# Score stage: up blocks multiplied in native fp32 from the raw weights

## The chip, the cores and the metric

The kernel runs on one NeuronCore of a Trainium2 chip. The metric is the time of one execution in microseconds (us) on the device. Five engines work side by side, each on its own instruction stream: TensorE (PE: matmuls, with the weight loads PEld listed apart), VectorE (DVE), ScalarE (ACT), GpSimd (POOL) and SyncE (SP, which here issues the large DMAs). They meet at semaphores.

## The reference, cut to what matters

The program is one layer of a diffusion backbone on 128 context and 256 latent tokens: a token mixer (projection, bidirectional scan, output projection), then a channel mixer called PEER. Only PEER matters here:

```
q  = (h @ w_query)  as 8 heads x 2 halves x 128
s1 = q[:, :, 0] . sub_keys[0]      s2 = q[:, :, 1] . sub_keys[1]     # 128 scores per half
top 16 of each half, 16x16 sums, top 16 of the sums -> idx, gates = softmax(top)
act = gelu(x . expert_u[idx])      out = sum_k act * gate * expert_v[idx]
```

There are 16,384 experts of width 2048. For the 128 context tokens the kernel gathers the rows of the chosen experts. For the 256 latent tokens it computes the products with all experts densely (128 "up" blocks of 128 experts: `gelu(expert_u @ h)`), and weighs them with a table of gates that is zero where an expert was not chosen.

## The kernel before

The part around the change begins at line 1565. Its weights come as blocks of 128 x 2048 fp32 (1 MB), numbered m in the order of use. Each block goes through two-slot rings, slot r = m % 2: `raw` (as loaded), `whi` (its high part in fp32r, a rounded form that TensorE multiplies in one go) and `wlo` (raw minus whi, also fp32r). The activations h are kept three times: `h2` in fp32, `hhi` and `hlo` as high and low part. One 128x128 piece of a block is multiplied as whi x hhi + whi x hlo + wlo x hhi, three matmuls; 16 pieces make a block, so 48 matmuls (`up_product`, L1553 to L1559, for the 256 latent tokens; `query`, L1804 to L1816, for all 384 tokens).

The score stage is blocks 0 to 35. For each of 8 heads there are four blocks (`PER_HEAD`): query, query, up, up; the parity of a head's blocks is 0, 1, 0, 1. After them come `UPRE` = 4 further up blocks (32 to 35, from `M_PRE` on). So 16 query blocks and 20 up blocks. The next stage (the scatter stage, blocks 36 to 67, from `M_SCAT` on) builds the gate table; then the remaining up blocks run in a loop (`rest`), and the down blocks after them.

What sets the order in the score stage:

- SP (L1571 to L1605) loads block m into `raw[m % 2]` once the semaphore `w_low` of that slot says that block m-2 is done with (L1574). It then spills the gelu output of block m-3 to DRAM, if that was an up block, and goes on to block m+1. It is in order.
- ACT (L1679 to L1702) copies, per head m = 4h: the query result of block m, then makes `whi` of block m+2 (`high_of`, L1547); the result of block m+1, then `whi` of m+3; then `gelu` of block m+2, `whi` of m+4, the two score copies (L1696), `gelu` of m+3, `whi` of m+5. `high_of` waits for the load of its block and for the product of block m-2. In head 0, four copies of the turned tokens (`htok`, L1688) stand ahead of the first gelu. After the last blocks, ACT takes the Exp of the gates (L1704).
- POOL (L1951) makes `wlo` of blocks 0 to 35 in turn (`low_of`, L1542); its increment of `w_low` is what PE waits for before the product, and what SP waits for before it overwrites `raw`. After block 35 it waits for the chosen indices and starts the gathers of expert rows.
- PE (L1831 to L1852) runs query, query, up, the six score matmuls (L1844), up; each product waits for `w_low` of its block. After the last up block, PE waits for the gates and transposes them (L1854 to L1860).
- DVE runs `choose(h)` for each head (L2019 to L2056, the top-k work), which begins when the two score copies of the head are there; after head 7 it writes `idx` (L2066), waits for the Exp and normalises the gates (L2070 to L2074). The dots with gathered rows (L2082) and everything in the scatter stage follow.

Of the kernel before, what the change touches and what calls it, by code (L numbers as in the profile page):

```python
# [29 lines left out]
KD = D // P  # L30
CTX, LAT = 128, 256
T = CTX + LAT
# [126 lines left out]
def build_program(nc, x_t, c_t, cols_in, tables_in, w_ada, w_in, w2a2, w_s, b_s, state_t, w_out, w_query,  # L159
# [9 lines left out]
    with ctx:  # L169
        ps = ctx.enter_context(nc.psum_tensor("ps", [P, 8, 512], F32))  # L170
# [141 lines left out]
        raw = sb(b_scope, "raw", [P, RING, KD, P])  # L312
# [1003 lines left out]
        raw = stack_right(w_scope, "raw2", [P, RING, KD, P])  # L1316
# [120 lines left out]
        PER_HEAD = 2 + UPH  # L1437
        M_PRE = PKH * PER_HEAD
        M_SCAT = M_PRE + UPRE
        M_REST = M_SCAT + USCAT  # L1440
        M_DOWN = NQ + NK
# [39 lines left out]
        h2 = carve(fa_, KD, T)  # L1481
# [36 lines left out]
        w_landed = [sem(f"w_landed{r}") for r in range(2)]  # L1518
        w_high = sem("w_high")
        w_low = [sem(f"w_low{r}") for r in range(2)]  # L1520
        prod = sem("prod")
        q_out, u_out = sem("q_out"), sem("u_out")
# [16 lines left out]
        evicted, turned_back, added_back = sem("evicted"), sem("turned_back"), sem("added_back")  # L1539
        stores_y = sem("stores_y")  # L1540

        def low_of(eng, ops, m):  # L1542
            r = m % 2
            eng.wait_ge(w_high.sem, m + 1)
            ops.tensor_tensor(wlo[:, r], raw[:, r], whi[:, r].bitcast(F32), ALU.subtract).then_inc(w_low[r].sem, 1)  # L1545

        def high_of(act, m):  # L1547
            r = m % 2
            act.wait_ge(w_landed[r].sem, 16 * (m // 2 + 1))
            act.wait_ge(prod.sem, m - 1)  # L1550
            nc.scalar.activation(whi[:, r], raw[:, r], ACT.Copy).then_inc(w_high.sem, 1)
# [13 lines left out]
        with nc.Block() as block:  # L1565
# [100 lines left out]
            def _(act):  # L1666
                def gelu(m, g):
                    act.wait_ge(prod.sem, m + 1)
                    if g >= 2:
                        act.wait_ge(spilled[g % 2].sem, 16 * (g // 2))  # L1670
                    nc.scalar.activation(act_f[:, g % 2], ps[:, 2 + g % 2, 0:LAT], ACT.Gelu_apprx_tanh).then_inc(u_out.sem, 1)
# [7 lines left out]
                for h in range(PKH):  # L1679
                    m = h * PER_HEAD  # L1680
# [44 lines left out]
                for i in range(SCAT):  # L1725
                    m, g, q = M_SCAT + 2 * i, U_SCAT + 2 * i, QUADS * i
# [58 lines left out]
                for tile in range(2):  # L1785
                    for c in range(4):
                        act.wait_ge(sums_ready.sem, 4 * tile + c + 1)
                        last = nc.scalar.activation(vg[1 + tile][:, c * 512:(c + 1) * 512], ps[:, 4 * tile + c, :], ACT.Square,
                                                    accum_out=tok_part[:, tile, c:c + 1])
# [11 lines left out]
            def _(pe):  # L1801
# [14 lines left out]
                    last.then_inc(prod.sem, 1)  # L1816

                def up(m, g):
                    pe.wait_ge(w_low[m % 2].sem, m // 2 + 1)
                    if g >= 2:  # L1820
                        pe.wait_ge(u_out.sem, g - 1)
                    up_product(pe, m % 2, ps[:, 2 + g % 2, 0:LAT])
# [8 lines left out]
                for h in range(PKH):  # L1831
                    m = h * PER_HEAD
# [46 lines left out]
                for i in range(SCAT):  # L1879
                    m, g, q = M_SCAT + 2 * i, U_SCAT + 2 * i, QUADS * i  # L1880
# [58 lines left out]
            @block.gpsimd  # L1939
            def _(pool):  # L1940
                def gather(rows, s, buf, landed):
                    nc.gpsimd.indirect_dma_start(out=buf, out_offset=None, in_=rows,  # L1942
                                                 in_offset=bass.IndirectOffsetOnAxis(ap=idx[:, s:s + 1], axis=0)
                                                 ).then_inc(landed.sem, 16)

                def gather_u(s):
                    if s >= 2:
                        pool.wait_ge(ug_used.sem, s - 1)
                    gather(u_rows, s, ug[s % 2], ug_landed[s % 2])

                for m in range(M_SCAT):  # L1951
                    low_of(pool, nc.gpsimd, m)
                pool.wait_ge(x_saved.sem, 16)
                pool.wait_ge(idx_ready.sem, 1)
                for s in range(FIRST_DOTS):
                    gather_u(s)
                low_of(pool, nc.gpsimd, M_SCAT)
                low_of(pool, nc.gpsimd, M_SCAT + 1)
                pool.wait_ge(slots_here.sem, 1)

                def gate_two(q):
                    pool.wait_ge(fa_mask.sem, q + 1)
                    a = (4 * q) % 8 + 2
                    f = fa[:, a:a + 2, :]
                    nc.gpsimd.tensor_tensor(
                        f, f, slot[:, 0, 4 * q + 2:4 * q + 4].rearrange("p (t o) -> p t o", o=1).to_broadcast([P, 2, NK]),
                        ALU.mult).then_inc(fa_pool.sem, 1)

                gate_two(0)
                gate_two(1)  # L1970
                s = FIRST_DOTS
                for i in range(SCAT):
                    q = QUADS * i
                    gate_two(q + 2)
                    gate_two(q + 3)
                    for _ in range(SCAT_DOTS):
                        gather_u(s)
                        s += 1
                    if i < SCAT - 1:
                        gate_two(q + 4)  # L1980
                        gate_two(q + 5)
                    low_of(pool, nc.gpsimd, M_SCAT + 2 * i + 3)
                while s < SLOTS:
                    gather_u(s)
                    s += 1
                pool.wait_ge(stage_out[0].sem, 16 * (SCAT // 8))
                pool.wait_ge(stage_out[1].sem, 16 * (SCAT // 8))
                for s in range(SLOTS):
                    if s >= 4:
                        pool.wait_ge(vg_used.sem, s - 3)  # L1990
                    gather(v_rows, s, vg[s % 4], vg_landed[s % 4])

            @block.vector
            def _(dve):
# [122 lines left out]
                def rest(it):  # L2117
                    for n in range(4):
                        r = n % 2
                        dve.wait_ge(w_high.sem, it * 4 + (M_REST + 2 + n + 1))  # L2120
                        nc.vector.tensor_tensor(wlo[:, r], raw[:, r], whi[:, r].bitcast(F32), ALU.subtract).then_inc(w_low[r].sem, 1)  # L2121
                        u = (SLOTS - REST + n) % 2
                        dve.wait_ge(ug_landed[u].sem, it * 32 + 16 * ((SLOTS - REST + n) // 2 + 1))
                        nc.vector.scalar_tensor_tensor(out=ug[u], in0=ug[u], scalar=1.0, in1=htok[:, :], op0=ALU.mult,  # L2124
                                                       op1=ALU.mult, accum_out=dots[:, bass.ds(it * 4 + (SLOTS - REST + n), 1)]
                                                       ).then_inc(ug_used.sem, 1)
# [30 lines left out]
                                                   op0=ALU.mult, op1=ALU.add).then_inc(vg_used.sem, 1)  # L2157

                def v_low(it, j, e):
                    dve.wait_ge(w_high.sem, it * 4 + (M_DOWN + 2 * j + 2 + e + 1))  # L2160
                    nc.vector.tensor_tensor(wlo[:, e], v_raw[(2 * j + 2 + e) % 4], whi[:, e].bitcast(F32), ALU.subtract).then_inc(w_low[e].sem, 1)  # L2161

                def period(it, j, first=False):
# [111 lines left out]
```

## Time and profile before

| | before |
|---|---|
| median of 3 runs | 3718.75 us (3710.18 to 3724.95) |
| the profiled execution's own time | 3716.84 us |
| its span | 3715.0 us |
| PE busy | 3205.8 us (86%), 19560 instructions |
| PEld busy | 2821.9 us (76%) |
| DVE busy | 2501.2 us (67%) |
| ACT busy | 1426.1 us (38%) |
| POOL busy | 820.6 us (22%) |
| mean granted TensorE clock | 0.93 of full speed |

The span is the profiler's window around the instructions of the one profiled execution; the execution's own time is 1.84 us longer. The score stage lies between about 1705 and 2007 us. A matmul's row shows the time until its end leaves the array, and matmuls are pipelined: what one costs is the distance between two starts, not its duration. A native fp32 matmul shows as two records of a MATMUL and two of a LDWEIGHTS under one line of the source, an fp32r matmul as one of each.

### The profile page before, as it was taken

What the parts mean: (1) busy time and instruction counts of PE and PEld (TensorE: products, weight loads), DVE (VectorE), ACT (ScalarE), POOL (GpSimd) and SP (SyncE); (2) the same over time, 40 slices, a digit from 0 to 9 for tenths busy, and PEclk for the clock granted to TensorE, in tenths of its full rate; (3) what the DMA queues carried; (4) which work ended last, traced back from release to release, by engine and by line L of the source; (5) the groups of instructions that cost most, each with busy time, mean ns of one, the idle gap of its engine ahead of it and who ended that gap; (6) DMA issues with size and microseconds to landing.
All of it is one profiled execution on the core that took longest, in us unless ns stands there. A gap on an engine that the chain in (4) does not pass through costs nothing.

```text
span 3715.0 us, 52988 instructions
## 1 busy us (share of the span) xinstructions
PE 3205.8 (86%) x19560; PEld 2821.9 (76%) x19560; DVE 2501.2 (67%) x3095; ACT 1426.1 (38%) x1763; POOL 820.6 (22%) x469
## 2 busy tenths in 40 slices
PE   7988998949999999596996666569999799999997
PEld 2337998938888889494996666569999788788776
DVE  6985553365554452635997766667777699999997
ACT  6874333333334331425333333223333333333333
POOL 0000000001000010202565443331111234434442
PEclk9999999969999995798998888789999899999998
DMA  9983333200000000223445567779999999999996
GB/s 379 420 355 111 124 125 112 91 4 4 3 3 3 6 1 2 79 102 115 151 152 180 208 230 247 236 260 386 377 359 361 371 415 417 417 417 417 417 417 255
DMA packets 207375, 810.66 MB, mean 218 GB/s; under 512 B 81472, under 2 KB 101056, under 8 KB 118336
## 3 DMA queue, kind: packets, MB, share of 16 engines
q1 hardware_dynamic: 170432, 541.14, 38.9%
q0 software_dynamic: 36864, 268.45, 18.3%
q8 instruction: 51, 0.84, 0.1%
q14 instruction: 28, 0.23, 0.0%
HBM read 769.16 MB, written 40.37 MB: 218 GB/s over the span
## 4 chain that ended last, share of the span: by engine, by line
DMA 20%; DVE 13%; PE 12%; issue 4%; ACT 3%; POOL 1%; SPq 0%; DVEq 0%; ACTq 0%
DMA work<-act_table 10%; DMA raw<-expert_u 5%; DMA x<-u_rows,idx 4%; DVE x L2093 4%; PE ps L1556 2%; DVE x L2082 2%; PE ps L1558 2%; PE ps L1557 2%; DVE work L2156 2%; DVE wlo L2121 2%; ACT whi L1751 1%; PE ps L1813 1%; PE ps L1814 1%; PE ps L1815 1%; DVE wlo L2161 1%
## 5 line engine op out<-in xcount | busy, mean ns | idle before, releaser
L1556 PE MATMUL ps<-hhi,whi 128*128 128x256 f32 x2048 | 595.9, 291 | 32.5 <-DVE wlo L2121 14.9
L1557 PE MATMUL ps<-hlo,whi 128*128 128x256 f32 x2048 | 586.2, 286 | 0.0
L1558 PE MATMUL ps<-hhi,wlo 128*128 128x256 f32 x2048 | 585.3, 286 | 0.0
L1909 PE MATMUL ps<-whi,hhi 128*128 128x512 f32 x1024 | 402.0, 393 | 40.4 <-DVE wlo L2161 20.8
L1556 PEld LDWEIGHTS ps<-hhi,whi 128*128 128x128 f32 x2048 | 401.3, 196 | 41.2 <-issue 29.0
L282 PE MATMUL ps<-hhi,whi 128*128 128x384 f32 x1056 | 357.6, 339 | 79.0 <-DVE hlo L1413 42.9
L1557 PEld LDWEIGHTS ps<-hlo,whi 128*128 128x128 f32 x2048 | 400.6, 196 | 0.0
L1558 PEld LDWEIGHTS ps<-hhi,wlo 128*128 128x128 f32 x2048 | 399.7, 195 | 0.0
L1910 PE MATMUL ps<-wlo,hhi 128*128 128x512 f32 x1024 | 399.7, 390 | 0.0
L1911 PE MATMUL ps<-whi,hlo 128*128 128x512 f32 x1024 | 399.4, 390 | 0.0
L1942 POOL DMA_INDIRECT work<-expert_v,idx x128 | 287.2, 2244 | 445.5 <-DVE work L2156 430.5
L284 PE MATMUL ps<-hhi,wlo 128*128 128x384 f32 x1056 | 355.8, 337 | 0.0
L283 PE MATMUL ps<-hlo,whi 128*128 128x384 f32 x1056 | 355.7, 337 | 0.0
L1545 POOL TENSOR_TENSOR wlo<-raw,whi 128x2048 fp32r<-128x2048 f32 x54 | 251.4, 4658 | 329.5 <-ACT whi L1675 189.4
L2156 DVE SCALAR_TENSOR_TENSOR work<-work,dots 128x2048 f32<-128x2048 f32 x127 | 297.6, 2344 | 0.1
L271 DVE TENSOR_TENSOR wlo<-raw,whi 128x2048 fp32r<-128x2048 f32 x90 | 206.9, 2305 | 121.2 <-ACT whi L265 121.2
L282 PEld LDWEIGHTS ps<-hhi,whi 128*128 128x128 f32 x1056 | 200.7, 190 | 82.8 <-issue 56.7
L1909 PEld LDWEIGHTS ps<-whi,hhi 128*128 128x128 f32 x1024 | 192.9, 188 | 88.9 <-DVE wlo L2161 29.5
L2121 DVE TENSOR_TENSOR wlo<-raw,whi 128x2048 fp32r<-128x2048 f32 x76 | 174.2, 2292 | 124.0 <-ACT whi L1751 124.0
L1942 POOL DMA_INDIRECT x<-u_rows,idx x128 | 124.7, 975 | 524.7 <-DVE x L2124 390.4
L1876 PE MATMUL ps<-x 128*128 128x128 f32 x512 | 97.1, 360 | 162.1 <-DVE x L2093 142.4
L2082 DVE SCALAR_TENSOR_TENSOR x<-x,htok 128x2048 f32<-128x2048 f32 x52 | 134.6, 2590 | 140.4 <-DMA x<-u_rows,idx 140.4
(299 smaller groups left out, 6693.6 us busy)
## 6 DMA issues: line engine op xcount, KB each, us to landing
raw<-expert_u SPq DMA_DIRECT2D x128, 1024.0 KB
z<-w_ada SPq DMA_DIRECT2D x72, 1024.0 KB, 15.4
raw<-expert_v SPq DMA_DIRECT2D x64, 1024.0 KB
work<-expert_v SPq DMA_DIRECT2D x64, 1024.0 KB
raw<-w_in SPq DMA_DIRECT2D x50, 1024.0 KB, 4.8
raw<-w_ada SPq DMA_DIRECT2D x24, 1024.0 KB, 14.5
raw<-w_out SPq DMA_DIRECT2D x16, 1024.0 KB, 4.7
raw<-w_query SPq DMA_DIRECT2D x16, 1024.0 KB
```

Of the source, the lines that this page charges most:

```text
L282: pe.matmul(bank, hi[:, k, :], hhi[:, k, :], start=(k == 0), stop=False)
L283: pe.matmul(bank, hi[:, k, :], hlo[:, k, :], start=False, stop=False)
L284: last = pe.matmul(bank, lo[:, k, :], hhi[:, k, :], start=False, stop=(k == KD - 1))
L1545: ops.tensor_tensor(wlo[:, r], raw[:, r], whi[:, r].bitcast(F32), ALU.subtract).then_inc(w_low[r].sem, 1)
L1556: pe.matmul(bank, whi[:, r, k, :], moving_hi, start=(k == 0), stop=False)
L1557: pe.matmul(bank, whi[:, r, k, :], moving_lo, start=False, stop=False)
L1558: last = pe.matmul(bank, wlo[:, r, k, :], moving_hi, start=False, stop=(k == KD - 1))
L1909: pe.matmul(bank, ah, vh[:, part], start=first, stop=False)
L1910: done = pe.matmul(bank, ah, vl[:, part], start=False, stop=False)
L1911: done = pe.matmul(bank, al, vh[:, part], start=False, stop=last)
L1942: nc.gpsimd.indirect_dma_start(out=buf, out_offset=None, in_=rows, in_offset=bass.IndirectOffsetOnAxis(ap=idx[:, s:s + 1], axis=0)).then_i ...
L2156: nc.vector.scalar_tensor_tensor(out=accs[:, :], in0=vg[n], scalar=dots[:, bass.ds(it * 4 + n, 1)], in1=accs[:, :], op0=ALU.mult, op1=ALU. ...
```

## The change

A block for which `whole(m)` holds (the up blocks among blocks 0 to 31, and blocks 32 to 35: 20 in all) is multiplied straight from `raw` and `h2`, both fp32, in 16 native fp32 matmuls. For these blocks ACT makes no high part and POOL no low part. PE waits for the load itself (`w_landed`), and `w_low`, by which SP learns that the slot of `raw` is free, is incremented by ACT at the head of the block's gelu, after the product. The counts of `w_high` that other waits use are lowered accordingly. Query blocks and all blocks from 36 on are as before.

```diff
--- before.py
+++ after.py
@@ -1539,13 +1539,23 @@
         evicted, turned_back, added_back = sem("evicted"), sem("turned_back"), sem("added_back")
         stores_y = sem("stores_y")
 
+        def whole(m):
+            return M_PRE <= m < M_SCAT or (m < M_PRE and m % PER_HEAD >= 2)
+
+        WHOLE = sum(whole(m) for m in range(M_DOWN))
+
+        def highs(m):
+            return sum(not whole(n) for n in range(m + 1))
+
         def low_of(eng, ops, m):
             r = m % 2
-            eng.wait_ge(w_high.sem, m + 1)
+            eng.wait_ge(w_high.sem, highs(m))
             ops.tensor_tensor(wlo[:, r], raw[:, r], whi[:, r].bitcast(F32), ALU.subtract).then_inc(w_low[r].sem, 1)
 
         def high_of(act, m):
             r = m % 2
+            if whole(m):
+                return
             act.wait_ge(w_landed[r].sem, 16 * (m // 2 + 1))
             act.wait_ge(prod.sem, m - 1)
             nc.scalar.activation(whi[:, r], raw[:, r], ACT.Copy).then_inc(w_high.sem, 1)
@@ -1666,6 +1676,8 @@
             def _(act):
                 def gelu(m, g):
                     act.wait_ge(prod.sem, m + 1)
+                    if whole(m):
+                        act.sem_inc(w_low[m % 2].sem, 1)
                     if g >= 2:
                         act.wait_ge(spilled[g % 2].sem, 16 * (g // 2))
                     nc.scalar.activation(act_f[:, g % 2], ps[:, 2 + g % 2, 0:LAT], ACT.Gelu_apprx_tanh).then_inc(u_out.sem, 1)
@@ -1816,6 +1828,15 @@
                     last.then_inc(prod.sem, 1)
 
                 def up(m, g):
+                    if whole(m):
+                        pe.wait_ge(w_landed[m % 2].sem, 16 * (m // 2 + 1))
+                        if g >= 2:
+                            pe.wait_ge(u_out.sem, g - 1)
+                        for k in range(KD):
+                            last = pe.matmul(ps[:, 2 + g % 2, 0:LAT], raw[:, m % 2, k, :], h2[:, k, CTX:T],
+                                             start=(k == 0), stop=(k == KD - 1))
+                        last.then_inc(prod.sem, 1)
+                        return
                     pe.wait_ge(w_low[m % 2].sem, m // 2 + 1)
                     if g >= 2:
                         pe.wait_ge(u_out.sem, g - 1)
@@ -1949,7 +1970,8 @@
                     gather(u_rows, s, ug[s % 2], ug_landed[s % 2])
 
                 for m in range(M_SCAT):
-                    low_of(pool, nc.gpsimd, m)
+                    if not whole(m):
+                        low_of(pool, nc.gpsimd, m)
                 pool.wait_ge(x_saved.sem, 16)
                 pool.wait_ge(idx_ready.sem, 1)
                 for s in range(FIRST_DOTS):
@@ -2117,7 +2139,7 @@
                 def rest(it):
                     for n in range(4):
                         r = n % 2
-                        dve.wait_ge(w_high.sem, it * 4 + (M_REST + 2 + n + 1))
+                        dve.wait_ge(w_high.sem, it * 4 + (M_REST + 2 + n + 1 - WHOLE))
                         nc.vector.tensor_tensor(wlo[:, r], raw[:, r], whi[:, r].bitcast(F32), ALU.subtract).then_inc(w_low[r].sem, 1)
                         u = (SLOTS - REST + n) % 2
                         dve.wait_ge(ug_landed[u].sem, it * 32 + 16 * ((SLOTS - REST + n) // 2 + 1))
@@ -2157,7 +2179,7 @@
                                                    op0=ALU.mult, op1=ALU.add).then_inc(vg_used.sem, 1)
 
                 def v_low(it, j, e):
-                    dve.wait_ge(w_high.sem, it * 4 + (M_DOWN + 2 * j + 2 + e + 1))
+                    dve.wait_ge(w_high.sem, it * 4 + (M_DOWN + 2 * j + 2 + e + 1 - WHOLE))
                     nc.vector.tensor_tensor(wlo[:, e], v_raw[(2 * j + 2 + e) % 4], whi[:, e].bitcast(F32), ALU.subtract).then_inc(w_low[e].sem, 1)
 
                 def period(it, j, first=False):
```

## Rows read from the trace of the kernel before

**Rows 1.** A stretch of the score stage: length; PE, PEld, DVE, ACT, POOL busy.

```profile
1800.00:1850.00 50.00, 50.00 (x344) 49.67 (x343) 47.18 (x131) 16.80 (x18) 30.18 (x8) 1.00 0.40 134
```

**Rows 2.** Timeline of ACT, one head: start, duration, line, work, idle before.

```profile
1847.51 0.38 ACT L1671 ACTIVATE act_f<-ps 128x256 f32<-128x256 f32 x1 [3.45 <-PE ps L1558]
1847.79 1.91 ACT L1551 ACTIVATE whi<-raw 128x2048 fp32r<-128x2048 f32 x1
1849.60 0.86 ACT L1696 ACTIVATE work<-ps 128x384 f32<-128x384 f32 x2
1854.85 0.38 ACT L1671 ACTIVATE act_f<-ps 128x256 f32<-128x256 f32 x1 [4.39 <-PE ps L1558]
...
1877.24 0.38 ACT L1671 ACTIVATE act_f<-ps 128x256 f32<-128x256 f32 x1 [3.45 <-PE ps L1558]
```

**Rows 3.** Timeline of PE: second matmul of an up block, then the scores.

```profile
1747.11 0.28 PE L1557 MATMUL ps<-hlo,whi 128*128 128x256 f32 x1
...
1752.74 1.50 PE L1844 MATMUL ps<-work 128*128 128x128 f32 x12
```

**Rows 4.** Timeline of PE in the scan: native fp32 matmuls, 256 columns.

```profile
837.34 0.59 PE L1127 MATMUL ps<-kr,z 128*128 128x256 f32 x2
...
838.21 0.38 PE L1127 MATMUL ps<-kr,z 128*128 128x256 f32 x1
```

**Rows 5.** Timeline of PE: native fp32 matmuls of 384 columns, back to back.

```profile
1698.64 2.23 PE L1297 MATMUL ps<-z,tab 128*128 128x384 f32 x6 [0.21 <-ACT z L1289]
```

**Rows 6.** Timeline of SP: one 1 MB load is issued.

```profile
1832.04 0.33 SPq L1569 DMA_DIRECT2D raw<-expert_u  x1
```

**Rows 7.** Stretches of 1 us after that issue; last column is GB/s.

```profile
1836.00:1837.00 1.00, 1.00 (x8) 1.00 (x7) 0.95 (x5) 0.00 (x0) 1.00 (x1) 1.00 0.24 98
1837.00:1838.00 1.00, 1.00 (x8) 1.00 (x7) 0.91 (x3) 0.00 (x0) 1.00 (x1) 1.00 0.00 0
```

**Rows 8.** Timeline of POOL: a low part, after its high part.

```profile
1849.78 4.63 POOL L1545 TENSOR_TENSOR wlo<-raw,whi 128x2048 fp32r<-128x2048 f32 x1 [1.04 <-ACT whi L1551]
```

**Rows 9.** Timeline of ACT in head 0.

```profile
1754.71 1.09 ACT L1688 ACTIVATE htok<-ps 128x512 f32<-128x512 f32 x2 [5.13 <-PE ps L1828]
```

**Rows 10.** Timeline of PE: starts after an idle time.

```profile
1763.98 0.69 PE L1813 MATMUL ps<-hhi,whi 128*128 128x384 f32 x1 [3.12 <-POOL wlo L1545]
...
1994.25 0.39 PE L1556 MATMUL ps<-hhi,whi 128*128 128x256 f32 x1 [1.78 <-POOL wlo L1545]
```

**Rows 11.** Stretches of PE after these starts; PEclk is the granted clock.

```profile
1764.00:1766.80 2.80, 2.80 (x9) 0.50 0.66 161
...
1995.60:1999.00 3.40, 3.40 (x18) 0.51 0.78 303
```

**Rows 12.** Timeline of DVE: choose(6) ends, choose(7) runs, gates follow.

```profile
1959.76 1.83 DVE L2040 TENSOR_TENSOR work<-work,tab 128x768 f32<-128x768 f32 x2
...
1970.39 1.26 DVE L2005 MAX8 work<-work 128x8 f32<-128x128 f32 x6 [0.29 <-DVE second L2054]
...
1988.81 6.20 DVE L2040 TENSOR_TENSOR work<-work,tab 128x768 f32<-128x768 f32 x2
...
1999.59 0.23 DVE L2066 CAST idx<-dots 128x128 uint32<-128x128 f32 x1
2005.83 0.55 DVE L2070 TENSOR_REDUCE rstd<-gates 128x24 f32<-128x384 f32 x1 [6.02 <-ACT gates L1704]
```

**Rows 13.** Timeline of ACT, from the first up block of head 7 on.

```profile
1966.42 0.38 ACT L1671 ACTIVATE act_f<-ps 128x256 f32<-128x256 f32 x1 [3.45 <-PE ps L1558]
...
2001.79 0.38 ACT L1671 ACTIVATE act_f<-ps 128x256 f32<-128x256 f32 x1 [6.86 <-PE ps L1558]
2002.07 1.90 ACT L1551 ACTIVATE whi<-raw 128x2048 fp32r<-128x2048 f32 x1
2003.98 1.28 ACT L1704 ACT_TABLE_LOAD   x1
2005.28 0.52 ACT L1704 ACTIVATE gates<-gates 128x384 f32<-128x384 f32 x1
```

## The prediction, made before the changed kernel was run

> **What bounds the kernel now.** I read the page's slices first (the score stage lies at 1705 to 2007 us), then the stretches of 50 us, then the timeline of each engine over one head. In a stretch inside the stage PE is busy 50.00 of 50 us at full clock, DVE 47.18, ACT 16.80 and POOL 30.18 [rows 1]; the two stretches after it look the same. So PE sets the pace and DVE is close behind. One head lasts from gelu to gelu 1877.24 - 1847.51 = 29.73 us, of which the stretch from the first up block's end to the second's is 1854.85 - 1847.51 = 7.34 [rows 2].
>
> What a block costs is read from distances of starts. From the second matmul of an up block to the score matmuls are 47 distances in 1752.74 - 1747.11 = 5.63 us [rows 3], so 0.1198 us each and 5.75 for 48. A query block is half of the rest of the head, (29.73 - 7.34 - 5.75) / 2 = 8.32. Of the 7.34, 5.75 is the second up block and 1.6 the score matmuls and their hand-over.
>
> **The change, part by part.** I call T the moment at which ACT sees the first up block of a head finished (1847.51 in rows 2).
>
> 1. The product. 48 fp32r matmuls become 16 native ones of 256 columns, 32 records. The scan has them in this width: two matmuls (four records, each with its own weights loaded beside the running product) take 838.21 - 837.34 = 0.87 us, so 0.2175 a record [rows 4]. Six records of 384 columns take (2.23 - 0.59) / 5 = 0.328 each [rows 5] (0.59 is the duration of one such record in the same stretch; five distances make the rest), and twelve of 128 columns 0.111 [rows 3]: 0.85 to 0.87 ns a column at three widths. A block is 32 x 0.2175 = 6.96 us, 1.21 more than 5.75. The ends: 32 x 0.2175 from the row of the same width is the low one; each of the four passes as dear as an fp32r matmul, 4 x 0.1198 x 16 = 7.67, the high one. I take 6.96, the row of the same shape.
>
> The Trainium skill ("FP8 and Floating Point Precision", TensorE Precision Notes) says that true fp32 takes 4 passes through the array. By that rule, with a pass priced as the fp32r matmul that the block uses today, the block is the 7.67 above, and it would be 1.92 dearer instead of 1.21. The trace agrees with four passes but prices them lower, at 0.435 us for a matmul [rows 4].
>
> 2. ACT's high part (1.91 us [rows 2]) and POOL's low part (4.63 [rows 8]) go, 20 times. Both lie beside PE's work, and for the query blocks they stay. Gain: nothing on the path. Of POOL's work beside choose(7) more below.
>
> 3. The release of `raw`. This is the term that counts. Today SP may reload a slot as soon as the low part is made, long before the product; now a whole block holds its slot until its product is over, and ACT frees it. Both up blocks of a head are followed in their slots by the next head's query blocks, which still need load, high part and low part. The load: issued at 1832.04 [rows 6], still 98 GB/s in the microsecond from 1836 and nothing from 1837 [rows 7], so landed after 4.2 to 4.3; with the two hand-overs 4.4. ACT starts the high part, POOL starts 1.99 later (1849.78 - 1847.79 [rows 2, 8]) and takes 4.63. The first query block of the next head is thus ready at T + 4.4 + 1.99 + 4.63 + 0.1 = T + 11.1. PE has the scores and the second up block in front of it, 1.6 + 6.96 = 8.56: it stands idle for some 2.5 us, in every head but the last. Behind the waiting product on PE stand only the rest of the next head's work, on ACT the score copies: these now wait for the load and the high part (T + 6.4 in place of T + 2.1), and choose(h) begins 4.3 later in its head. DVE has the room for that, since the head gets longer by more.
>
> The second query block: its slot is free at T + 8.56, so it is ready at T + 19.66; PE ends the first at 11.1 + 8.32 = T + 19.42. A tie, 0.24 of idle time. Then 8.32 + 6.96 and 0.25 of hand-over: the head lasts 35.2 us, 5.5 more than 29.73.
>
> 4. The clock. After an idle time of 3.12 us the first query block of head 1 ran at a granted clock of 0.50 for 2.80 us [rows 10, 11]; after one of 1.78 the granted clock fell to 0.51 for 3.40 us, a little later [rows 10, 11]. Idle times of 2.5 lie between these. 2.8 us at half clock lose 1.4 us. In a head that has it, the first query block ends at T + 20.8, the tie of part 3 is gone, and the head lasts 20.8 + 8.32 + 6.96 + 0.25 = 36.35, 6.6 more. Ends for this part: 5.5 (no head loses) to 6.6 or, with two such stretches, 8.0. I take 6.6 in five heads and 5.5 in one.
>
> 5. Head 0. Here ACT frees the slot only after the last two `htok` copies, which end at 1754.71 + 1.09 = 1755.80 [rows 9], and these come 1.21 later for the dearer up block: 1757.0. The query block starts at 1757.0 + 11.1 = 1768.1, against 1763.98 [rows 10], and the clock is low after it in both. With 1.21 for the next up block, T of head 1 is 5.3 late.
>
> 6. The end of the stage. Seen from T of head 7 (1966.42), DVE begins to normalise the gates at 2005.83 [rows 12, 13], 39.4 later. There the chain is: last product, seen at 2001.79, a high part for block 37, the table load and the Exp [rows 13]. New: 1.6 + 5 x 6.96 = 36.4 for the product. The high part of block 37 stands ahead of the Exp on ACT, and its slot is free only now: 4.4 for the load, 1.95 for the high part, 1.28 + 0.55 for table and Exp: 44.6. That is 5.2 late. The whole blocks among these (32 to 35) need the load alone, which takes less than one product, so PE does not wait.
>
> choose(7) gets shorter: with POOL at work its two L2040 take 6.20 us, without 1.83 [rows 12]. It also begins sooner, so `idx` is there some 20 us before the gates. It buys little: the first dots stand behind the gates on DVE (2005.83 comes after `idx` at 1999.59 [rows 12]), and the gathers after the first two wait for the dots.
>
> Sum: 5.3 (head 0 and the up block after it) + 5 x 6.6 + 5.5 (heads 1 to 6) + 5.2 = 49.0 us. From the gates on, everything hangs on them or on `idx`; loads and gathers of the next stage stand to the gates as before, so I see nothing that takes the delay up. 3716.84 + 49.0 = 3765.8 for the profiled execution; the median of the runs stands 1.9 above that, so **3768 us**.
>
> **Rivals.**
>
> *Dearer passes or more half clock (slower still).* If a block is 7.67, 0.71 more, this adds 2 x 0.71 before head 1, 0.71 in each of six heads (the second up block lies under the reload) and 5 x 0.71 at the end: 9.2, so 3777. If each of seven stalls costs two half-clock stretches, 7 x 1.4 = 9.8: 3778. For it: a block reads h2 and raw in fp32, which no row shows in this stage, and rows 10 have a stretch of half clock after only 1.78 idle. Against it: three widths agree on the price. This is also the case of the skill's rule in part 1.
>
> *The reload is hidden.* If the slot came free early, or load and split took under 8.5 us together, only the arithmetic is left: 15 x 1.21 = 18.2 before T of head 7, and at the end 36.4 + 0.4 + 1.9 + 1.85 = 40.6 against 39.4: 1.2. Then 3718.75 + 19.4 = 3738. For it: PE has 8.56 us of work in front, and 2.5 is not much to be wrong by. Against it: load, high and low part are in series, each from a row.
>
> *DVE sets the pace (faster).* DVE is busy 47 of 50 us, and choose(7) begins 0.29 after choose(6), without a wait for the scores [rows 1, 12]. If the top-k chain is what holds each head, and PE's full rows only hide waiting, taking POOL's work from beside it gives back 6.20 - 1.83 = 4.4 a head, 8 x 4.4 = 35: 3684. It decides from the point where PE's head fits into DVE's, some 25 us. Against it: PE's head is 8.32 x 2 + 5.75 x 2 + 1.6 = 29.7 by its own starts, the whole period, and becomes 32.2 even without a stall. The Trainium skill ("SBUF — State Buffer", Who interferes with whom) calls the port pair that DVE and GpSimd share an exclusive lock, held for a whole instruction. The trace agrees, with 6.20 against 1.83, but on an engine that does not end last.
>
> **How the numbers follow.** Forecast 0.70; the slower-still case 0.17; hidden reload 0.08; DVE 0.03; something else 0.02, mostly slower. The forecast's own range is 3759 (no half clock at all, 43.5 less what the runs scatter) to 3775. To hold 8 in 10 it takes in the slower-still case and leaves the hidden reload out: 3746 to 3786. Half a per cent, 18.6 us, is about what a measurement here can tell from no change; the hidden reload lies just on that line and is shared out. Slower 0.92, same 0.05, faster 0.03.
>
> **What would show it.** Up products of 32 records at 0.2175 us, about 6.96 from start to start of their neighbours. PE idle about 2.5 us before the first query block of each head from 1 to 7 (5 us in head 1's case), ended by POOL's low part, whose high part was ended by a DMA on `raw`; SP's issues for those blocks right behind the gelu and not behind POOL. Heads of 35 to 36.5 us. A granted clock below 1.00 in the stage. DVE idle before each choose. ACT waiting for a load before the Exp. The stages after it as long as before. It is wrong if PE goes from the second up block straight into the next query block, if records of 256 columns stand far from 0.2175 apart, or if the scatter stage is shorter by what the score stage lost.

## The result and the profile after

The changed kernel takes 3770.09 us (median of 4 runs, 3753.49 to 3779.54) against 3714.47 for the kernel before on the same chips (4 runs, 3701.62 to 3724.95). The ratio is 1.0147, 95% interval 1.0097 to 1.0196, so slower by 36 to 73 us; 3768 had been forecast. That the two times lie 2 us apart is partly luck: the forecast added 49.0 us to a median of 3718.75, while the two medians here are 55.6 us apart and start from 3714.47. The profiled execution of the changed kernel is the slowest of its four (3779.54, span 3777.6). Its distance to the profile of before (62.6 us of span) is more than the distance of the medians, and the stages have to be read one by one.

L and a number is a line of the kernel that ran. In the changed kernel L1836 is the native product, L1825 the first matmul of a query piece, L1683 the gelu, L1561 and L1553 the high and the low part, L1579 the load, L1695 the copy of a query result.

The stretches of the score stage, in the order length; PE, PEld, DVE, ACT, POOL busy; granted clock, DMA share, GB/s (before: [rows 1]):

```profile
1800.00:1850.00 50.00, 43.50 (x218) 40.99 (x217) 36.06 (x139) 9.41 (x13) 18.14 (x4) 0.93 0.39 137
1850.00:1900.00 50.00, 46.41 (x251) 43.59 (x250) 37.34 (x131) 7.32 (x10) 9.19 (x3) 1.00 0.32 111
```

PE was busy all the time before; now it stands idle 3.6 to 6.5 us in 50, and DVE has room. ACT over one head (against [rows 2]):

```profile
1793.33 0.38 ACT L1683 ACTIVATE act_f<-ps 128x256 f32<-128x256 f32 x1 [6.50 <-PE ps L1836]
1798.12 1.91 ACT L1561 ACTIVATE whi<-raw 128x2048 fp32r<-128x2048 f32 x1 [4.41 <-DMA raw<-w_query]
1799.94 0.85 ACT L1708 ACTIVATE work<-ps 128x384 f32<-128x384 f32 x2
1801.58 0.38 ACT L1683 ACTIVATE act_f<-ps 128x256 f32<-128x256 f32 x1 [0.78 <-PE ps L1836]
1806.63 1.91 ACT L1561 ACTIVATE whi<-raw 128x2048 fp32r<-128x2048 f32 x1 [4.67 <-DMA raw<-w_query]
...
1830.17 0.38 ACT L1683 ACTIVATE act_f<-ps 128x256 f32<-128x256 f32 x1 [6.50 <-PE ps L1836]
```

The high part followed the gelu at once before (0.28 us from start to start [rows 2]). Now ACT waits 4.41 us for the load of the first query block, with the score copies behind it, and again 4.67 us for that of the second. The head lasts 1830.17 - 1793.33 = 36.84 us. The load on SP, then stretches of 1 us after it, then POOL and PE (against [rows 6, 7, 8, 10]):

```profile
1793.28 8.57 SPq L1579 DMA_DIRECT2D raw<-w_query  x2
```

```profile
1797.00:1798.00 1.00, 1.00 (x6) 0.90 (x5) 0.00 (x0) 0.00 (x0) 0.00 (x0) 1.00 0.32 131
1798.00:1799.00 1.00, 1.00 (x6) 0.87 (x6) 0.00 (x0) 0.88 (x1) 0.00 (x0) 1.00 0.00 0
```

```profile
1800.11 4.51 POOL L1553 TENSOR_TENSOR wlo<-raw,whi 128x2048 fp32r<-128x2048 f32 x1 [24.81 <-ACT whi L1561]
```

```profile
1804.68 0.44 PE L1825 MATMUL ps<-hhi,whi 128*128 128x384 f32 x1 [3.23 <-POOL wlo L1553]
...
1841.58 0.45 PE L1825 MATMUL ps<-hhi,whi 128*128 128x384 f32 x1 [3.28 <-POOL wlo L1553]
```

The chain is to be read as one line: ACT sees the first up block done at T = 1793.33, SP has issued the reload at 1793.28, ACT starts the high part at 1798.12 (4.8 later), POOL the low part 1.99 after that, and PE starts the query block at T + 11.35, after 3.23 us of idle time. The granted clock right behind it, on PE alone (length, PE busy, granted clock, DMA share, GB/s):

```profile
1804.70:1808.30 3.60, 3.60 (x12) 0.56 0.98 382
1808.60:1813.90 5.30, 5.30 (x32) 1.00 0.15 59
```

This half clock does not come in every head. Two heads later the start and the idle time are much the same, and the clock stays full (the row at 1914.31 is one head on, with half clock again):

```profile
1878.35 0.45 PE L1825 MATMUL ps<-hhi,whi 128*128 128x384 f32 x1 [3.11 <-POOL wlo L1553]
...
1914.31 0.69 PE L1825 MATMUL ps<-hhi,whi 128*128 128x384 f32 x1 [3.11 <-POOL wlo L1553]
```

```profile
1878.40:1882.00 3.60, 3.60 (x21) 1.00 1.01 394
```

Of the six heads, four ran the first query block at half clock at its start (at 1804.68, 1841.58, 1914.31 and 1951.06) and two did not (at 1878.35 and 1987.88). From its start to the copy of its result it took 10.2 us in the four and 8.6 in the two.

The end of the stage, on ACT (against [rows 13], where the last head's first gelu was at 1966.42 and the Exp at 2005.28). 2012.17 is the last head's first up block:

```profile
2012.17 0.38 ACT L1683 ACTIVATE act_f<-ps 128x256 f32<-128x256 f32 x1 [6.50 <-PE ps L1836]
...
2034.23 0.38 ACT L1683 ACTIVATE act_f<-ps 128x256 f32<-128x256 f32 x1 [6.53 <-PE ps L1836]
2041.14 0.38 ACT L1683 ACTIVATE act_f<-ps 128x256 f32<-128x256 f32 x1 [6.52 <-PE ps L1836]
2050.61 1.91 ACT L1561 ACTIVATE whi<-raw 128x2048 fp32r<-128x2048 f32 x1 [9.09 <-DMA raw<-expert_u]
2052.43 0.36 ACT L1683 ACTIVATE act_f<-ps 128x256 f32<-128x256 f32 x1
2055.78 1.91 ACT L1561 ACTIVATE whi<-raw 128x2048 fp32r<-128x2048 f32 x1 [2.99 <-DMA raw<-expert_u]
2057.71 1.28 ACT L1716 ACT_TABLE_LOAD   x1
2059.00 0.52 ACT L1716 ACTIVATE gates<-gates 128x384 f32<-128x384 f32 x1
```

Two loads now stand ahead of the Exp, 9.09 and 2.99 us of waiting. And POOL's first gather, which before followed `idx` at 1999.59 [rows 12], is issued while PE still has two blocks to go:

```profile
2038.05 1.15 POOL L1963 DMA_INDIRECT x<-u_rows,idx  x1 [41.55 <-DVE idx L2088]
2039.50 0.94 POOL L1963 DMA_INDIRECT x<-u_rows,idx  x1 [0.30 <-issue]
```

### The profile page after: what moved, and what is told of

The parts are those of the page before. It is cut to its first block, busy times and chain, and to the rows that moved or that the text cites. A ratio compares the mean times of both kernels' runs of the same rounds, so it can differ in the third digit from the quotient of the medians.

```text
span 3777.6 us, 52233 instructions
## 1 busy us (share of the span) xinstructions
PE 3237.1 (86%) x19240; PEld 2829.8 (75%) x19240; DVE 2469.4 (65%) x3095; ACT 1394.2 (37%) x1743; POOL 758.0 (20%) x449
## 4 chain that ended last, share of the span: by engine, by line
DMA 24%; DVE 12%; PE 9%; issue 4%; ACT 3%; POOL 2%; SPq 1%; DVEq 0%; ACTq 0%
DMA work<-act_table 10%; DMA raw<-expert_u 9%; DMA x<-u_rows,idx 4%; DVE x L2115 3%; PE ps L1836 3%; DVE wlo L2143 2%; DVE x L2104 2%; ACT whi L1763 2%; DVE work L2178 2%; DVE wlo L2183 1%; DMA raw<-w_query 1%; POOL wlo L1553 1%; PE ps L1825 1%; PE ps L1827 1%; PE ps L1826 1%
## 5 line engine op out<-in xcount | busy, mean ns | idle before, releaser
L1566 PE MATMUL ps<-hhi,whi 128*128 128x256 f32 x1728 | 504.9, 292 | 35.9 <-DVE wlo L2143 17.2
L1567 PE MATMUL ps<-hlo,whi 128*128 128x256 f32 x1728 | 494.2, 286 | 0.0
L1568 PE MATMUL ps<-hhi,wlo 128*128 128x256 f32 x1728 | 493.4, 286 | 0.0
L1930 PE MATMUL ps<-whi,hhi 128*128 128x512 f32 x1024 | 402.1, 393 | 36.8 <-DVE wlo L2183 18.4
L1963 POOL DMA_INDIRECT work<-expert_v,idx x128 | 310.5, 2425 | 416.4 <-DVE work L2178 398.6
L1566 PEld LDWEIGHTS ps<-hhi,whi 128*128 128x128 f32 x1728 | 337.4, 195 | 47.7 <-issue 37.6
L1567 PEld LDWEIGHTS ps<-hlo,whi 128*128 128x128 f32 x1728 | 337.1, 195 | 0.0
L1568 PEld LDWEIGHTS ps<-hhi,wlo 128*128 128x128 f32 x1728 | 336.2, 195 | 0.0
L282 PEld LDWEIGHTS ps<-hhi,whi 128*128 128x128 f32 x1056 | 200.7, 190 | 83.0 <-issue 56.7
L1553 POOL TENSOR_TENSOR wlo<-raw,whi 128x2048 fp32r<-128x2048 f32 x34 | 158.8, 4674 | 426.1 <-ACT whi L1561 236.9
```

Source lines behind the costliest of these rows:

```text
L282: pe.matmul(bank, hi[:, k, :], hhi[:, k, :], start=(k == 0), stop=False)
L1566: pe.matmul(bank, whi[:, r, k, :], moving_hi, start=(k == 0), stop=False)
L1567: pe.matmul(bank, whi[:, r, k, :], moving_lo, start=False, stop=False)
L1568: last = pe.matmul(bank, wlo[:, r, k, :], moving_hi, start=False, stop=(k == KD - 1))
L1930: pe.matmul(bank, ah, vh[:, part], start=first, stop=False)
```

## Where the time went, stage by stage

Three numbers per kernel carry the comparison; all are starts of rows. "Head" is the mean distance of the first gelus of heads 1 to 7, over six heads. "End" is from the last head's first gelu to DVE's first work on the gates. "Stage" is from ACT's copy of block 1's result (1746.32 before, 1746.70 after, ahead of which nothing differs) to the first matmul of the gate table; it is given as the difference to the kernel before, 2028.2 - 1746.3 = 281.9. "Whole" is the median of the kernel's runs; it was taken beside runs of the kernel before whose medians were 3714.47 (for the changed kernel), 3711.98 (own_slots and hold_only) and 3715.39 (candidate). Where there was one run only, its time is given and says little by itself.

| kernel | head | end | stage | whole, us |
|---|---|---|---|---|
| before | 29.73 | 39.4 | 0 | 3714.47 |
| changed | 36.47 | 47.4 | +53.7 | 3770.09 |
| own_slots | 31.82 | 47.2 | +23.4 | 3742.14 |
| hold_only | 36.31 | 56.6 | +57.7 | 3758.97 |
| heads_only | 36.40 | 44.4 | +54.1 | 3752.59 (one run) |
| further_only | 29.72 | 46.4 | +7.3 | 3718.76 (one run) |
| filler | 35.63 | 47.4 | +47.4 | 3775.64 (one run) |
| first_only | 37.43 | 42.4 | +55.9 | 3748.89 (one run) |
| second_only | 35.63 | 45.2 | +42.0 | 3766.73 (one run) |
| gathers_later | 36.38 | 44.8 | +50.8 | 3753.56 (one run) |
| exp_early | 36.42 | 31.2 | +41.0 | 3771.53 (one run) |
| candidate | 29.71 | 30.4 | -4.8 | 3713.12 |

After the first matmul of the gate table the changed kernel repeats the kernel before: the last one starts at 2454.2 before and 2508.4 after, the table stage taking 426.0 and 426.1 us. The loop of up blocks behind it (first to last low part of DVE) is another matter. The line's summary in four kernels, columns: count, duration min/median/max in ns, first and last start. Before, changed, heads_only and exp_early in turn, all with the same code there, which is L2121 in the kernel before:

```profile
L2121 DVE TENSOR_TENSOR wlo<-raw,whi x76: 2287/2292/2294, 2491.1 to 2943.1; 128x2048 fp32r<-128x2048 f32 x76
```

```profile
L2143 DVE TENSOR_TENSOR wlo<-raw,whi x76: 2286/2293/2294, 2547.3 to 3010.2; 128x2048 fp32r<-128x2048 f32 x76
```

```profile
L2143 DVE TENSOR_TENSOR wlo<-raw,whi x76: 2285/2292/2293, 2550.3 to 2983.3; 128x2048 fp32r<-128x2048 f32 x76
```

```profile
L2144 DVE TENSOR_TENSOR wlo<-raw,whi x76: 2290/2293/2295, 2531.4 to 3003.0; 128x2048 fp32r<-128x2048 f32 x76
```

These are 452.0, 462.9, 433.0 and 471.6 us. Over the profiles of all twelve kernels the loop takes 433.0 to 471.6 us: 433.0 to 435.6 in four of the five whose stage was delayed by 50 us or more, 462.9 in the fifth, which is the changed kernel, and 449.7 to 471.6 in the other seven. So a late score stage does not by itself make the loop longer. Whether the loop's length hangs on when it begins or varies from one execution of a kernel to the next is open, since no kernel was profiled twice. I take the 10.9 us that the changed kernel's profile has here in excess as no part of the change, and the 53.7 of the stage as the change, which the 55.6 between the medians fits. Between the table and the loop the changed kernel takes 2.0 us more and behind the loop 4.5 us less.

## The experiments

**own_slots.** The up blocks of the heads go to slots of their own, in memory that is free by then; the query blocks keep `raw` and their counts get semaphores of their own. POOL also waits for both new slots before its first gather. The cut below is shortened, its last two lines are in words.

```diff
+own_raw = [xf[:, n * D:(n + 1) * D].rearrange("p (k c) -> p k c", k=KD) for n in range(2)]
 ...
-load(m, r, (w_query if kind == "q" else expert_u)[n])
+if kind == "q": wait q_low[r] >= m // 4; load raw[:, r]       # free after the low part
+else:           wait own_free[r] >= m // 4; load own_raw[r]   # free after the product
```

> The changed kernel, but the 16 up blocks of the heads get two slots of their own (the memory of x, which is free once x is saved), so that a query block can be loaded while the up block before it is still being multiplied. The product stays native. Theory (the reload causes the idle time): PE goes from the second up block straight into the next query block, a head lasts 2 x 8.32 + 2 x 6.96 + 1.6 = 32.2 us in place of the 36.5 of the changed kernel, the granted clock stays at 1.00, the last head's first up block is some 17 us later than in the kernel before instead of 46, and the whole is about 3714 + 25 = 3740 us. Rival (the native product itself, or something beside it, makes the head longer): heads stay at 36 to 37 us and the whole at 3770.

Measured: 3742.14 us, 1.0067 of the kernel before (1.0030 to 1.0104). ACT's first gelus of two heads following, then all engines over 50 us (as in [rows 1]):

```profile
1795.40 0.38 ACT L1712 ACTIVATE act_f<-ps 128x256 f32<-128x256 f32 x1 [6.50 <-PE ps L1872]
1795.68 1.90 ACT L1574 ACTIVATE whi<-raw 128x2048 fp32r<-128x2048 f32 x1
...
1827.22 0.38 ACT L1712 ACTIVATE act_f<-ps 128x256 f32<-128x256 f32 x1 [6.50 <-PE ps L1872]
```

```profile
1800.00:1850.00 50.00, 50.00 (x275) 47.93 (x274) 41.44 (x161) 8.80 (x11) 15.95 (x4) 1.00 0.45 161
```

The high part follows the gelu at once again, PE is busy 50.00 of 50 at full clock, and the head lasts 31.82. So of the 6.74 us by which a head grew, 4.65 go with the late reload (with what it costs in clock) and 2.09 stay with the native products. The rival, by which the heads would stay at 36 to 37 us, is out. Heads (31.82) and whole (3742.14) are close to the 32.2 and 3740 that were expected.

**hold_only.** The kernel before, all products in three parts, with one more wait on SP:

```diff
     sp.wait_ge(w_low[r].sem, m // 2)
+    if M_PRE <= m - 2 < M_SCAT or (m - 2 < M_PRE and (m - 2) % PER_HEAD >= 2):
+        sp.wait_ge(prod.sem, m - 1)
```

> The kernel before with one edit: the load that follows one of the 20 up blocks in its slot waits for that block's product and not for its low part. All products stay three fp32r matmuls. Theory (holding the slot is the cost, and the dearer second up block lies under the wait): PE idle 4 us before the first query block of a head, heads of 35 to 36 us, last head's first up block about 38 us later than before; at the end of the stage the four further up blocks now wait for load, high and low part, 50 us to the gates against 39.4; together about +49, 3763 us. Rival (the arithmetic is the larger part): at most +20, 3735 us.

Measured: 3758.97 us, 1.0155 (1.0083 to 1.0226), and +57.7 at the end of the stage. ACT at a head's end and the PE row behind it, then a later head's PE row with the stretch that follows:

```profile
1824.47 0.38 ACT L1673 ACTIVATE act_f<-ps 128x256 f32<-128x256 f32 x1 [3.45 <-PE ps L1558]
1829.22 1.92 ACT L1551 ACTIVATE whi<-raw 128x2048 fp32r<-128x2048 f32 x1 [4.37 <-DMA raw<-w_query]
```

```profile
1835.79 0.69 PE L1815 MATMUL ps<-hhi,whi 128*128 128x384 f32 x1 [4.03 <-POOL wlo L1545]
...
1907.83 0.69 PE L1815 MATMUL ps<-hhi,whi 128*128 128x384 f32 x1 [4.14 <-POOL wlo L1545]
```

```profile
1907.90:1913.00 5.10, 5.10 (x16) 0.50 0.85 277
```

Without a single native product in it the stage gets as long as with all 20 of them, a little longer even. So the late release alone is enough for a loss of this size. The equality is partly chance, for three things come together:

- The second up block is hidden. It is 1.2 us shorter here, and the query block still starts 11.3 to 11.5 us after T (11.2 to 11.4 in the changed kernel); the difference is idle time (4.0 to 4.3 us in place of 3.1 to 3.3).
- The first up block is not hidden. It too is 1.2 us shorter (5.75 us from the last query copy to its gelu, in place of 6.99), and this should have made the head 1.2 us shorter. But behind the longer idle time the half clock came in all six heads and lasted longer, up to 5.1 us as in the row above: the first query block took 10.1 to 11.5 us, 10.8 on average, in place of 9.7. This takes back most of what the cheaper block saved, and the head is 36.31 against 36.47.
- The end is 56.6, since the four further blocks here need load, high and low part in series. This had been put at 50.

The whole is 47 us above the kernel before of the same session, against 57.7 at the end of the stage; the loop of up blocks took only 433.8 us in this profile.

**first_only and second_only.** `whole(m)` returns true for one of a head's two up blocks.

```diff
-    return M_PRE <= m < M_SCAT or (m < M_PRE and m % PER_HEAD >= 2)
+    return m < M_PRE and m % PER_HEAD == 2        # second_only: == 3
```

> Only the first up block of each head is whole, the second and the further four are split. Theory (one late reload is enough to stretch the head): the first query block is ready 11.5 us after the first up block's end, PE has 7.35 of work, so heads of 36 to 37 us, as with both. If the loss goes by the number of whole blocks: half of it, heads of 33.

> Only the second up block of each head is whole. Theory: the first query block is ready in time, the second one is ready 11.4 to 11.8 us after the second up block's end and PE has 8.32 of work: idle 3.3, then half clock; heads of 34.5 to 36 us. If the loss goes by the number of whole blocks: 33. If the second slot's reload is harmless, since in the changed kernel it was a tie: 31.

Heads of 37.43 and 35.63 us. Either block alone costs about as much as the two together (36.47): the two late reloads overlap, and what one loses hides the other. The loss does not go by the number of changed blocks, and the tie of the second slot in the changed kernel was no sign that this slot is harmless. In second_only PE waits 3.4 to 3.5 us for the second query block, as expected.

First_only came out above its 36 to 37 us. The rows say where the extra 1 us is: the first query block starts at T + 11.3 as in the changed kernel, but its own time is 10.8 us on average in place of 9.7. The second up block is the short one, so PE is idle 4.2 to 4.4 us instead of 3.1 to 3.3, and the half clock behind it comes in every head and lasts longer:

```profile
1840.64 0.69 PE L1825 MATMUL ps<-hhi,whi 128*128 128x384 f32 x1 [4.42 <-POOL wlo L1553]
```

```profile
1840.70:1845.50 4.80, 4.80 (x16) 0.53 0.77 246
```

**heads_only and further_only.** `whole(m)` for the 16 blocks of the heads, or for the 4 further ones.

```diff
-    return M_PRE <= m < M_SCAT or (m < M_PRE and m % PER_HEAD >= 2)
+    return m < M_PRE and m % PER_HEAD >= 2        # further_only: M_PRE <= m < M_SCAT
```

> The changed kernel, with the 16 up blocks of the heads whole and the 4 further ones split as before. Theory: the heads last as in the changed kernel (36.5 us) and the last head's first up block is 46 us late; from there to the gates 42 to 43 us (39.4 before, 47.4 in the changed kernel), since the Exp no longer stands behind a load of block 37 that begins only after a product. At the gates about +49 us. If the end of the stage costs nothing of its own: the same +54 as the changed kernel.

> The counterpart: only the 4 further up blocks are whole, the heads as before. Theory: heads of 29.7 us, the last head as in the kernel before, and from its first up block to the gates 44 to 47 us in place of 39.4, so +4.5 to +7.5 at the gates, by the dearer products, less the stalls on POOL's low parts that they remove, and the load of block 37 ahead of the Exp. Rival (the end of the stage is neutral): 39 to 41 us.

At the first matmul of the gate table the heads carry 54.1 and the further blocks 7.3, which is more than the 53.7 of both. At the gates, where the forecasts were put, it is 51.2 for heads_only (about 49 forecast) and 6.9 for further_only (4.5 to 7.5 forecast), against 53.3 for both. In heads_only the end is 44.4 (42 to 43 forecast): its split blocks wait up to 3.4 us for low parts behind late reloads. Further_only has 46.4, inside its range.

**filler.** PE gets work into a bank that nobody reads, while it would wait.

```diff
+if h:
+    for n in range(16):
+        pe.matmul(ps[:, 6, 0:T], hhi[:, n, 0:P], hhi[:, n, :], start=(n == 0), stop=(n == 15))
 query(m, 2 * h)
```

> The changed kernel, with 16 fp32r matmuls of 384 columns (2.8 us, into a bank that nobody reads) on PE ahead of the first query block of heads 1 to 7, where PE stands idle for some 3.2 us. Theory (part of the longer head is half clock after that idle time): no stretch of half clock in the heads, each lasts 35.4 to 35.7 us in place of 36.5 on average. Rival (the clock plays no part, the reload alone sets the head): 36.5, or longer by what the filler overruns.

PE over 220 us of the heads (length, PE busy, granted clock, DMA share, GB/s), the filler's kernel first, the changed one second; then the start of a query block with the filler ahead of it:

```profile
1780.00:2000.00 220.00, 216.98 (x1162) 1.00 0.35 122
```

```profile
1780.00:2000.00 220.00, 200.41 (x1041) 0.97 0.35 121
```

```profile
1800.82 0.45 PE L1825 MATMUL ps<-hhi,whi 128*128 128x384 f32 x1 [0.44 <-POOL wlo L1553]
```

Idle time in front of the query block falls to 0.34 to 0.48, the granted clock stays at 1.00, and a head is 0.84 us shorter on average, 35.63 against 36.47. Its heads of 35.54 to 35.74 are close to the two heads of the changed kernel that kept full clock (35.60 and 35.95). With useless work added the stage ends 6.3 us sooner. The half clock after an idle time is thus a real term, about 6 of the 54. What decides whether it comes is open: in the changed kernel one idle time of 3.11 us was followed by it and another of 3.11 us was not.

**gathers_later.** POOL waits for the load of block 36 before its first gather.

```diff
 pool.wait_ge(idx_ready.sem, 1)
+pool.wait_ge(w_landed[0].sem, 16 * (M_SCAT // 2 + 1))
```

> The changed kernel, with POOL's first gathers held until block 36 has landed. Theory (the load of block 36 took 9.4 us and not 4.8 because two gathers of 1 MB, issued 3 us before it, ran beside it): it lands after 4.8, ACT sees the last further up block 2 to 3 us sooner, and from the last head's first up block to the gates are 44.5 to 45 us in place of 47.4. Rival (the load was slow for another reason): 47.4.

The issue of block 36's load on SP, and the high part that waits for it on ACT:

```profile
2040.78 0.33 SPq L1579 DMA_DIRECT2D raw<-expert_u  x1
```

```profile
2047.74 1.91 ACT L1561 ACTIVATE whi<-raw 128x2048 fp32r<-128x2048 f32 x1 [6.53 <-DMA raw<-expert_u]
```

From issue to high part it is 7.0 us, against 9.5 in the changed kernel (2041.09 to 2050.61), and the end is 44.8. The gathers cost 2.5 us. That it is still 7.0 and not the 4.8 that had been expected is not explained; a spill of 128 KB is issued right behind the load, and no run separates the two.

**exp_early.** The Exp moves ahead of the high part of block 36.

```diff
     gelu(M_PRE + n, U_PRE + n)
+    if n == UPRE - 2:
+        act.wait_ge(chosen.sem, 1)
+        nc.scalar.activation(gates, gates, ACT.Exp).then_inc(gates_exp.sem, 1)
     high_of(act, M_PRE + n + 2)
-act.wait_ge(chosen.sem, 1)
-nc.scalar.activation(gates, gates, ACT.Exp).then_inc(gates_exp.sem, 1)
```

> The changed kernel, with ACT's Exp of the gates moved ahead of the high part of block 36. Theory (at the end of the stage the Exp waits on ACT behind the loads of blocks 36 and 37, which begin only after a product): DVE starts on the gates some 32 us after the last head's first up block in place of 47.4, the transposes then wait for PE's last product, and the first matmul of the gate table comes 10 to 14 us sooner than in the changed kernel. Rival (the last product or the load itself holds the gates): no change.

```profile
2041.92 0.38 ACT L1683 ACTIVATE act_f<-ps 128x256 f32<-128x256 f32 x1 [6.52 <-PE ps L1837]
2042.33 1.28 ACT L1716 ACT_TABLE_LOAD   x1
2043.62 0.52 ACT L1716 ACTIVATE gates<-gates 128x384 f32<-128x384 f32 x1
2051.25 1.91 ACT L1561 ACTIVATE whi<-raw 128x2048 fp32r<-128x2048 f32 x1 [7.11 <-DMA raw<-expert_u]
```

The gates are taken 31.2 us after the last head's first up block in place of 47.4, and the table begins 12.7 us sooner (+41.0 against +53.7), both as expected. So the loads did stand ahead of the gates through ACT's order alone. The whole took 3771.53 us in its one run, and its loop of up blocks took 471.6 us: a single time hides the effect.

**candidate.** further_only with the Exp moved.

> A version meant to beat both: only the four further up blocks whole (which takes POOL's work from beside the last top-k) and the Exp moved ahead of the high part of block 36. Theory: heads as before, idx some 7 us sooner than before (1992.8 against 1999.6), gates at about 1998 in place of 2005.8, PE's last product at 2001, first matmul of the gate table 5 to 9 us sooner than before; 3712 - 7 = 3705 us, which is hardly more than a measurement can tell. Rival (the scatter stage takes its pace from something else): same as before.

3713.12 us (12 runs) against 3715.39 (17), ratio 0.9987 (0.9962 to 1.0013): no difference that can be measured; 3705 had been expected. In its profile the stage is 4.8 us shorter than before, just short of the 5 to 9 expected. It was not shown to beat the kernel before.

## Why the prediction was right, point by point

- *The product.* Forecast 6.96 us for a block. Two gelus of the further blocks lie 2041.14 - 2034.23 = 6.91 apart. The row of the same shape in another stage had the price. The Trainium skill ("FP8 and Floating Point Precision", TensorE Precision Notes) says four passes and no price; the 7.67 that came of pricing each pass as an fp32r matmul is what the 6.91 rules out. With slots of their own these products cost 2.09 us a head, against the 2.4 of the forecast.
- *The release of the slot.* Forecast T + 11.1 for the query block, measured T + 11.35. The load is the part that was off: 4.8 from issue to use instead of 4.4, while the low part took 4.51 instead of 4.63. The traffic ends at about 1797.6 (82 GB/s in the 0.2 us before, none after), which is near the 4.2 to 4.3 that [rows 6, 7] had shown; ACT starts 0.5 after that. I had read the end of the traffic as the landing. PE was idle 3.1 to 3.3 us and not 2.5: besides the 0.25, its work in front took 8.1 us and not 8.56.
- *That the second up block lies under the reload.* hold_only shows it by the start of the query block, which stays at T + 11.3 to 11.5 with a second up block 1.2 us shorter. That its head comes within 0.2 us of the changed kernel's is no proof of this, since the first up block lies on the path and only a longer half clock made up for it.
- *The tie of the second slot.* In the head above its load took 5.1 us from issue to use and it was ready at T + 19.9, while PE, slowed by the clock, came free at about T + 21.4. It did not count, as forecast for heads with half clock. In the two heads with full clock it did: PE waited up to 0.49 us there, against 0.24 in the forecast.
- *The clock.* Forecast 6.6 more in five of six heads and 5.5 in one. The heads are 36.84, 36.95, 35.95, 36.75, 36.75, 35.60: 6.74 more on average against 6.4. Half clock came in four of them, not five, and cost 1.6 us each time, not 1.4. Both kinds of head were longer than forecast (about 36.8 against 36.35, and 35.8 against 35.2). The filler shows that the half clock is a cause; the split of five to one came from no row, and that the average is so close is in part luck.
- *Head 0.* Query block at 1768.05, forecast 1768.1. This stage began 0.38 us later in the changed kernel's profile, so that against it the block was 0.4 sooner than forecast, and T of head 1 was 4.9 late and not 5.3.
- *The end of the stage.* This term was mis-sized: 47.4 against 44.6 forecast, 8.0 more than before and not 5.2. I had written that the earlier `idx` "buys little". It costs: it lets two gathers run beside the load of block 36, on which ACT waits with the last gelu and the Exp behind it. gathers_later takes 2.6 of the 2.8 us away. The waits that the forecast had named, load and high part of block 37 ahead of the Exp, are there too.
- *Sum.* 49.0 forecast, 53.7 measured at the gate table, 55.6 between the medians. The 4.7 between the first two are 2.8 at the end of the stage, 2.0 in the six heads (40.5 against 38.5) and 0.4 between the gates and the table, less 0.4 ahead of the heads. What lies between 53.7 and 55.6 is within the scatter of the runs.
- *The rivals.* The hidden reload is what own_slots makes true: +23.4, against 19.4 worked out. The DVE rival falls: DVE is busy 36 to 37 of 50 in the two stretches shown and 37 to 41 in own_slots, with POOL busy 9 to 18 us of 50 in these stretches against 30 [rows 1], and the head is longer all the same. What this rival built on is real (the two L2062 of the last top-k took 1.83 us without POOL beside them, against 6.20 with it [rows 12]) but lies off the path, where the earlier `idx` even did harm.

## What to carry to other kernels

Before dropping a copy or a split, ask what else it did: here the split was the hand-over that freed the load buffer one product earlier, and in a head this was worth twice as much as the arithmetic (4.65 us against 2.09). Work out the reload as a chain (product end, issue, landing, each step until the consumer can start) and compare it with the work that PE has in front; here PE was fully busy with two slots, so the excess became idle time, and in four of six heads the idle time brought half clock behind it. On an engine that runs in order, look at which waits stand ahead of the next stage's first operation.

## What was not expected

- The loop of the remaining up blocks takes between 433.0 and 471.6 us with the same code. This is nearly as wide as the scatter of the whole (3693 to 3736 us for the kernel before in 13 runs); that the loop is the source of that scatter is not shown. Effects of 5 to 13 us in another stage are seen in that stage's rows and not in the total.
- A reload of 1 MB in the heads of the changed kernel is usable 4.7 to 5.4 us after the gelu that frees its slot (4.7 to 4.9 for the first slot, 5.0 to 5.4 for the second), some 0.5 us after its traffic ends where this was looked at.
- A low part on POOL can hold up even a very small DVE operation: the conversion of 96 numbers a partition (L2048) took 4.33 us when it met a low part (started at 1992.23, with the low part from 1991.89 to 1996.50), and 0.21 when there was none. It does not hold up every operation: six MAX8 (L2027) took 1.26 us beside a low part at 1910.68, and 1.26 at 2014.15 with none.
